# Third norm taken on token rows, router logits from the raw residual, and the first expert's rows gathered by 0/1 matmuls in a two-layer hybrid decoder step

## What is computed

```python
def layer_norm(x, g, b):
    mu = jnp.mean(xf, axis=-1, keepdims=True)
    var = jnp.mean(jnp.square(xf - mu), axis=-1, keepdims=True)
    y = (xf - mu) * lax.rsqrt(var + LN_EPS) * g + b

def moe_swiglu(x, w_router, w_gu, w_down):
    logits = (x @ w_router).astype(jnp.float32)
    top_v, top_i = lax.top_k(logits, TOP_K)
    gates = jax.nn.softmax(top_v, axis=-1)
    ...
    for e in range(N_EXPERTS):
        y = y + swiglu(x, w_gu[e], w_down[e]) * combine[..., e:e + 1]
```

## Time and profile before

| | |
|---|---|
| median of 3 runs | 1705.26 us (1704.07 to 1706.66) |
| the profiled execution's own time | 1708.3 us |
| its span | 1706.4 us |
| PE busy, matmuls / weight loads | 1584.2 us / 1377.1 us |
| DVE / ACT / POOL busy | 1245.2 / 1058.4 / 92.0 us |
| output projection's last matmul ends | at 639.86 us |
| first expert matmul starts | at 688.17 us |

### The profile page before, as it was taken

The page is one execution under the profiler, slowest core; times in us unless marked ns, Lnnn a source line. Parts: engine busy times, 40 slices in busy tenths (PEclk is TensorE's granted clock), DMA queues, the critical chain, the costliest instruction groups (busy, mean ns, idle before and its releaser), DMA issues.

```text
span 1706.4 us, 23448 instructions
## 1 busy us (share of the span) xinstructions
PE 1584.2 (93%) x8917; PEld 1377.1 (81%) x8917; DVE 1245.2 (73%) x1155; ACT 1058.4 (62%) x976; POOL 92.0 (5%) x142
## 2 busy tenths in 40 slices
PE   7999998799996994999999999999999999999992
PEld 6889997699996994787887887887887887887881
DVE  5685444467544653688888888888888888888887
ACT  3981414566434334677877777777777777777772
POOL 3104100011000002000000000000000000002001
PEclk9997998899998997899999999999999999999996
DMA  9646702489552552799999999999999999999991
GB/s 254 212 137 200 279 2 87 131 270 298 203 187 75 173 174 103 280 376 364 360 380 343 382 376 338 391 367 346 390 365 351 385 367 351 384 366 352 396 376 71
DMA packets 228128, 479.65 MB, mean 281 GB/s; under 512 B 9644, under 2 KB 69052, under 8 KB 227769
## 3 DMA queue, kind: packets, MB, share of 16 engines
q1 hardware_dynamic: 215904, 438.92, 72.0%
q0 software_dynamic: 10640, 37.96, 6.4%
q10 hardware_dynamic: 1528, 1.98, 0.4%
...
...
## 4 chain that ended last, share of the span: by engine, by line
PE 87%; ACT 6%; DVE 4%; DMA 1%; issue 1%; POOL 0%; DVEq 0%; SPq 0%; ACTq 0%; POOLq 0%
PE bank L1741 12%; PE bank L1742 12%; PE bank L1745 12%; PE bank L1770 11%; PE bank L342 6%; PE bank L343 6%; PE bank L347 6%; PE bank L1776 6%; ACT high L323 2%; PE bank L1656 1%; PE bank L1657 1%; PE bank L1525 1%; PE bank L1662 1%; PE bank L1546 1%; DVE low L328 1%; PE bank L1753 1%
## 5 line engine op out<-in xcount | busy, mean ns | idle before, releaser
L328 DVE TENSOR_TENSOR low<-raw,high 128x2048 fp32r<-128x2048 f32 x408 | 932.7, 2291 | 279.3 <-ACT high L323 279.3
L323 ACT ACTIVATE high<-raw 128x2048 fp32r<-128x2048 f32 x408 | 781.9, 1918 | 297.2 <-PE bank L1745 108.0
L1741 PE MATMUL bank<-high,xgh 128*128 128x512 f32 x896 | 360.4, 402 | 1.6 <-DVE xgl L1328 1.6
L1742 PE MATMUL bank<-high,xgl 128*128 128x512 f32 x896 | 356.4, 398 | 0.0
L1745 PE MATMUL bank<-low,xgh 128*128 128x512 f32 x896 | 246.7, 397 | 0.0
L342 PE MATMUL bank<-xh,high 128*128 128x264 f32 x864 | 231.0, 300 | 16.8 <-ACT xh L774 9.3
L343 PE MATMUL bank<-xl,high 128*128 128x264 f32 x864 | 227.6, 296 | 0.0
L1745 PEld LDWEIGHTS bank<-low,xgh 128*128 128x128 f32 x896 | 169.8, 190 | 41.2
L1741 PEld LDWEIGHTS bank<-high,xgh 128*128 128x128 f32 x896 | 169.9, 190 | 40.5 <-issue 2.0
L1742 PEld LDWEIGHTS bank<-high,xgl 128*128 128x128 f32 x896 | 169.5, 189 | 38.6
L342 PEld LDWEIGHTS bank<-xh,high 128*128 128x128 f32 x864 | 173.2, 200 | 19.3 <-ACT xh L774 9.7
(11 more groups left out here) (347 smaller groups left out, 1424.6 us busy)
## 6 DMA issues: line engine op xcount, KB each, us to landing
...
```

Of the source, the lines that this page charges most:

```text
L323: eng.activation(high[:, n % SPLIT, :], raw[:, n % RAW, :], ACT.Copy).then_inc(high_ready, 1)
L328: eng.tensor_tensor(low[:, n % RAW, :], raw[:, n % RAW, :], high[:, n % SPLIT, :].bitcast(F32), ALU.subtract).then_inc(low_ready, 1)
L1741: pe.matmul(out, xgh[:, 4 * kh + k, :], wh[:, k, :], start=kh + k == 0, stop=False)
L1742: pe.matmul(out, xgl[:, 4 * kh + k, :], wh[:, k, :], start=False, stop=False)
```

## The change

It does the following.

- **Norm on rows.** PE transposes the un-normed residual into token rows (`row_tiles`, 24 transposes): the first 12 ahead of the last output slot, 6 after it, 6 after the last residual add. DVE takes mean and variance of each row with `bn_stats` (`row_stats`), ACT computes the inverse root, DVE the product `nmr`, and ACT writes `xn` = row * rstd + nmr, without gain and bias. `layer_norm(2)` goes.
- **Logits from the raw residual.** POOL multiplies the router's weights by the norm's gain and bias once, early (`gbw`); PE sums them over the channels with 8 matmuls against ones (`sgb`), ahead of the output slots; the logits are (raw residual x `gbw`) * rstd + nmr * `sgb` part + bias part.
- **First expert by matmul.** DVE compares seat numbers with each token's seat of expert 0 (`onehot`, 0/1), and 24 fp32 matmuls `xn` x `onehot` put the rows into the banks where the transposes of `xrow` used to. The scatter stays, and SP waits for it only at unit 3 of the first job.
- **Gain and bias later.** `tok` now holds rows without gain and bias, so `gathered` first multiplies and adds on DVE (`xf`, 8 operations for each of the jobs), then ACT copies and DVE subtracts. DVE also makes `acc` (6 operations) just before the loop, where ACT did it in one.
- **Filler.** `keep_running` issues transposes of the identity whose results nobody reads: 24, 12 and 20 of them.
- **Rest.** DVE's `low` for the loop's third slot moves behind the ranking; ACT's program has explicit table loads ahead of its norms, before `deltaT`, and at the end; POOL loads gain and bias rows in the short convolution's stage, where ACT did so after the third norm; the last `flag` operation waits for `y_sb` instead of the stored `ysb`.

```diff
                     last = pe.matmul(out, wl[:, k, f], act_h[:, k, :], start=False, stop=k == KT - 1)
             last.then_inc(slot_used, 1)
 
...
+                            sp_.wait_ge(scattered, 96)
...
+            sp_.dma_start(tok[bass.ds(final + 1, 1), :, :].rearrange("a p d -> p (a d)"), ysb[:, :]).then_inc(y_last, 16)
...
+            for i in range(2):
+                pool.wait_ge(ss_out[i], 64)
+            pool.wait_ge(tail_out, 32)
+            for l, at in ((0, vec2_g), (1, vec_g)):
+                pool.dma_start(at[:, :], ln_g[1, l:l + 1, :].to_broadcast([128, D])).then_inc(vec_in, 16)
+            for l, at in ((0, vec2_b), (1, vec_b)):
+                pool.dma_start(at[:, :], ln_b[1, l:l + 1, :].to_broadcast([128, D])).then_inc(vec_in, 16)
+            for a in range(2):
+                ins = pool.tensor_tensor(gbw[:, :, a, :], wr[:, :, :], vecs[:, :, 4 * a + 2:4 * a + 3].to_broadcast([128, KT, EX]),
+                                         ALU.mult)
+            ins.then_inc(const_ready, 1)
...
-            pool.wait_ge(slot_used, MOE0)
+            pool.wait_ge(yl_ready, 8)
...
+            pool.wait_ge(slot_used, MOE0)
...
+            pool.wait_ge(y_sb, final * 2 + 4)
             step(pool.tensor_tensor(flag[:, 3:4], flag[:, 0:1], flag[:, 1:2], ALU.add))
             step.wait()
+            pool.wait_ge(y_last, 16)
...
             act.activation(zgate[:, :, :], zgate[:, :, :], ACT.Copy, scale=norm_w[:, 0:1]).then_inc(z_ready, 1)
...
@@ -826,28 +860,26 @@
             for n in range(SCO0, MOE0):
                 act.wait_ge(slot_used, n + 1)
                 split_high(act, n + SPLIT)
...
-            layer_norm(2, False)
-
-            act.dma_start(vec_g[:, :], ln_g[1, 1:2, :].to_broadcast([128, D])).then_inc(vec_in, 16)
-            act.dma_start(vec_b[:, :], ln_b[1, 1:2, :].to_broadcast([128, D])).then_inc(vec_in, 16)
-            act.wait_ge(pool_step, 4 + 2 * LEVELS + 5)
-            for i in range(6):
-                act.wait_ge(xn_psum, i + 1)
-                p = 128 if i < 4 else 8
-                act.activation(xn[0:p, i // 2, 512 * (i % 2):512 * (i % 2) + 512], bank[i][0:p, :], ACT.Copy)\
-                    .then_inc(xn_ready, 1)
+            act.preload_act_table_set("natural_log")
+            act.wait_ge(var_ready, 1)
+            act.activation(rstd_n[:, :], moments[:, :, 1], ACT.Ln, bias=eps[:, 1:2]).then_inc(log_ready, 1)
+            act.wait_ge(log_ready, 1)
+            act.activation(rstd_n[:, :], rstd_n[:, :], ACT.Exp, scale=-0.5).then_inc(rstd_ready, 1)
+            act.wait_ge(nmr_ready, 1)
+            act.wait_ge(const_ready, 8)
+            for tt in range(3):
+                for h in range(2):
+                    p = 128 if tt < 2 else NS
+                    act.activation(xn[0:p, tt, 512 * h:512 * h + 512], bank[row_bank(tt, h)][0:p, :], ACT.Identity,
+                                   scale=rstd_n[0:p, tt:tt + 1], bias=nmr[0:p, tt:tt + 1]).then_inc(xn_ready, 1)
             act.wait_ge(top_ready, 1)
             act.activation(gates[:, :, :], gates[:, :, :], ACT.Exp).then_inc(ex_ready, 1)
-            act.wait_ge(xn_ready, 6)
-            act.activation(acc[:, :, :], xn[:, :, :], ACT.Copy, scale=ALPHA).then_inc(acc_ready, 1)
 
             def gathered(jobs):
                 for g in range(2):
-                    act.wait_ge(xg_psum, jobs * 2 + (g + 1))
-                    act.activation(xgh[:, 4 * g:4 * g + 4, :], heads(2 + g), ACT.Copy).then_inc(xgh_ready, 1)
-
-            act.wait_ge(scattered, 96)
-            act.dma_start(xrow[:, :], tok[1]).then_inc(xrow_in, 16)
...
@@ -1239,17 +1272,42 @@
                     dve.tensor_tensor(yl[:, f, :], sy[:, 2 * (i % 2) + t, :], yh[:, f, :].bitcast(F32), ALU.subtract)\
                         .then_inc(yl_ready, 1)
                 split_low(dve, n + SPLIT)
+            def row_stats(h):
+                for tt in range(3):
+                    p = 128 if tt < 2 else NS
+                    dve.wait_ge(xn_psum, 3 * h + tt + 1)
+                    step(dve.bn_stats(stats[0:p, tt, h, :], bank[row_bank(tt, h)][0:p, :]))
+
             for n in range(SCO0, MOE0):
                 dve.wait_ge(slot_used, n + 1)
                 for t in range(2):
                     add_residual(2 * (n - SCO0) + t, 2 * ((n - SCO0) % 2) + t)
-                split_low(dve, n + SPLIT)
-            layer_norm(2, False)
-
+                if n < MOE0 - 1:
+                    split_low(dve, n + SPLIT)
+                if n == SCO0:
+                    dve.wait_ge(sgb_psum, 1)
+                    step(dve.tensor_copy(sgb[:, :, :], bank[7][:, 0:16].rearrange("p (a e) -> p a e", a=2)))
+                if n == SCO0 + 2:
+                    row_stats(0)
+            dve.wait_ge(const_ready, 8)
+            row_stats(1)
+            step.wait()
+            for tt in range(3):
+                p = 128 if tt < 2 else NS
+                ins = dve.bn_aggr(moments[0:p, tt, :], stats[0:p, tt, :, :].rearrange("p g s -> p (g s)"))
+            ins.then_inc(var_ready, 1)
+            dve.wait_ge(var_ready, 1)
+            dve.wait_ge(rstd_ready, 1)
+            dve.scalar_tensor_tensor(nmr[:, :], moments[:, :, 0], -1.0, rstd_n[:, :], ALU.mult, ALU.mult).then_inc(nmr_ready, 1)
+            dve.wait_ge(nmr_ready, 1)
+            for tt in range(3):
+                step(dve.scalar_tensor_tensor(over[:, 0, tt, :], sgb[:, 0, :], nmr[:, tt:tt + 1], sgb[:, 1, :], ALU.mult, ALU.add))
             dve.wait_ge(logit_psum, 1)
-            dve.wait_ge(const_ready, 7)
-            step(dve.tensor_copy(logits[:, 0:2, :], bank[6][:, 0:16].rearrange("p (t e) -> p t e", t=2)))
-            step(dve.tensor_copy(logits[0:8, 2, :], bank[6][0:8, 16:24]))
+            step.wait()
+            for tt in range(3):
+                p = 128 if tt < 2 else NS
+                step(dve.scalar_tensor_tensor(logits[0:p, tt, :], bank[2][0:p, 8 * tt:8 * tt + 8], rstd_n[0:p, tt:tt + 1],
+                                              over[0:p, 0, tt, :], ALU.mult, ALU.add))
             step.wait()
             step(dve.tensor_reduce(top[:, :], logits[:, :, :], X, ALU.max))
...
+            step(dve.tensor_reduce(most[:, 0:1], bank[3][:, 24:32], X, ALU.max))
             step.wait()
             for k in range(1, TILES):
...
             step(dve.tensor_tensor(first_at[:, :, :], first_at[:, :, :], last_at[:, :, :], ALU.add))
             step(dve.tensor_reduce(row_f[:, 1, :], last_at[:, :, :], X, ALU.max))
             step.wait()
...
+                    dve.wait_ge(xg_psum, jobs * 2 + (g + 1))
+                    for d in range(4 * g, 4 * g + 4):
+                        ins = dve.tensor_scalar(xf[:, d, :], heads(2 + g)[:, d % 4, :], vecs[:, d, 2:3], vecs[:, d, 6:7],
+                                                ALU.mult, ALU.add)
+                    ins.then_inc(xf_ready, 1)
+                for g in range(2):
                     dve.wait_ge(xgh_ready, jobs * 2 + (g + 1))
-                    dve.tensor_tensor(xgl[:, 4 * g:4 * g + 4, :], heads(2 + g), xgh[:, 4 * g:4 * g + 4, :].bitcast(F32),
+                    dve.tensor_tensor(xgl[:, 4 * g:4 * g + 4, :], xf[:, 4 * g:4 * g + 4, :], xgh[:, 4 * g:4 * g + 4, :].bitcast(F32),
                                       ALU.subtract).then_inc(xgl_ready, 1)
 
             gathered(0)
+            for tt in range(3):
+                step(dve.scalar_tensor_tensor(acc[:, tt, :], xn[:, tt, :], ALPHA, vec2_g[:, :], ALU.mult, ALU.mult))
+            step.wait()
+            for tt in range(3):
+                step(dve.scalar_tensor_tensor(acc[:, tt, :], vec2_b[:, :], ALPHA, acc[:, tt, :], ALU.mult, ALU.add))
             tiles = dve.value_load(rounds_i[0:1, 0:1], min_val=1, max_val=TILES)
             with dve.Fori(0, tiles) as t:
...
                     pe.wait_ge(res_ready, 16 + 2 * i - 2)
+                if i == 3:
+                    pe.wait_ge(stail_sb, 2)
+                    row_tiles(0)
+                    row_tiles(2)
                 dense_slot(pe, n, 2 * (i % 2), yh, yl)
-            pe.wait_ge(stail_sb, 2)
-            layer_norm(2)
-
-            pe.wait_ge(x_new, 24)
+            pe.wait_ge(res_ready, 22)
+            row_tiles(4)
+            pe.wait_ge(res_ready, 24)
+            row_tiles(6)
             for tt in range(3):
                 n_tok = 128 if tt < 2 else NS
                 for k in range(KT):
-                    last = pe.matmul(bank[6][0:n_tok, 8 * tt:8 * tt + 8], xres[:, k, 128 * tt:128 * tt + n_tok], wr[:, k, :],
+                    last = pe.matmul(bank[2][0:n_tok, 8 * tt:8 * tt + 8], xres[:, k, 128 * tt:128 * tt + n_tok], gbw[:, k, 0, :],
                                      start=k == 0, stop=k == KT - 1)
             last.then_inc(logit_psum, 1)
-            for i in range(6):
-                tt, n_tok = i // 2, (128 if i < 4 else NS)
-                for t in range(4):
-                    last = pe.transpose(bank[i][0:n_tok, 128 * t:128 * t + 128],
```

(19 more changed lines are left out.)

67 lines of the change are left out of this document (54 added, 13 removed).

## The result

The changed kernel takes **1690.86 us** (median of 4 runs, 1687.96 to 1691.15) against 1705.68 (median of 4, 1704.07 to 1706.66): a ratio of **0.9911, 95% interval 0.9897 to 0.9925**, a gain of 14.8 us (12.8 to 17.6). The forecast was 1677, with a range of 1669 to 1688. The sign was right. The size was not, and the result lies 3 us outside the range.

The account below looks back on a forecast made before the run. TensorE, with 87% of the chain, was taken as the bound, losing most in a 48.3 us chain before the expert loop. Savings of 21.9 + 2.3 + 1.3 + 2.7 = 28.2 us from 1705.26 gave 1677, range 1669 to 1688.

Parts of the forecast that it names:

- sign: Whole kernel: faster, chance 0.95; same 0.02, slower 0.03.
- 0/1 matmuls, "5.4, to 20.9": First expert's 48 passes take 5.4 us, ending 20.9 us after the last output slot's end.
- Rival 2: Filler doesn't count: after the logits the clock stays at 0.50 into the 0/1 matmuls; 7 us less, 1684; chance 0.2.
- Chain up to the 0/1 matmuls, 15.5: From the last output slot's end through logits, ranking, filler and counts to the 0/1 matmuls: 15.5 us.
- Rule on the filler: The skill's rule that full clock does not engage for transposes; by it the filler would hold nothing.
- Clock at the loop's start, 2.3 us "taken whole": Expert loop's start: about 12 matmuls no longer at half clock, 12 x 0.2 = 2.3 us saved.
- Ahead of the last slot, -3.0: `sgb` sums (1.7 us) and 12 transposes (1.3 us) make the last output slot end 3.0 us later.
- Loop, zero: Expert loop's job ends: added `xf` operations cost nothing, 3.7 us of slack covering them with 0.6 us left.
- Rivals 3, 4 and 5: Job ends stall a little, 1681 to 1685 (0.13); slower there, 1713 (0.03); no gain in the stage, 1701 (0.02).
- DeltaNet, 1.3: DeltaNet stage: one table load of 1.28 us leaves the way to the copy of `P`, 1.3 us saved.
- Tail, 2.7: Program's end: the flag operation starts with the last store, so the gather starts earlier, 2.7 us saved.

Follow-up runs that it names:

- e5_no_filler: The changed kernel with the 0/1 matmuls over 128 rows (e2_full_rows), without any of the 56 filler transposes; 1690.64 us, ratio 0.9906.
- e2_full_rows: The changed kernel with the third token tile's 0/1 matmuls over all 128 rows instead of 8; 1682.37 us, ratio 0.9863.
- e6_before_tail: The kernel before with the change's last part alone, the flag computed while y is being stored; 1703.1 us, ratio 0.998.
- e12_before_tail_again: e6_before_tail measured again beside new runs of the kernel before; 1706.11 us against 1706.39, ratio 0.9994.

## Why the prediction was off, point by point

- **0/1 matmuls, "5.4, to 20.9": failed.** It took 13.32 us, because the price was taken from products over 128 rows while a third of the passes have 8. Over 128 rows the same term measures 5.60. These 7.9 us, the filler's half-clock passes behind it, which end 1.3 us beyond the last `xgl`, and an `xgl` that is done 2.8 us after the last pass and not 2.5, are the 9.6 us by which the chain is too long. None of the rivals had it. Rival 2 had a similar number (1684) and a low clock in the 0/1 matmuls too, but from filler that doesn't count, which `e5_no_filler` excludes; its counts, 18 passes at 0.156, are 2.8 us and not 3.1.
- **Chain up to the 0/1 matmuls, 15.5: right,** 15.57, and in part by luck. The clock fell in the middle of the logits, at 639.1, as reasoned from the decode stage. But the logits took 5.0 us where 6.0 had been counted, and the filler behind them 5.0 where 4.1 had been, so that it ends at 11.5 (forecast 11.6). `sel` is ready at 644.94, 9.95 us after the slot's end (forecast 10.9), and the counts start at 646.32: the filler holds them back by 1.4 us, twice the 0.7 of the forecast.
- **Rule on the filler: the trace decides against it here.** The clock came back 4.4 us into the first filler, when TensorE had issued nothing but `pe.transpose` of the identity since the logits, and without filler 8.3 us are lost. The Trainium skill, "TensorE: Matmul & The Clock Gate", Part 4, says that full clock doesn't engage for transposes; with these fp32 transposes it did.
- **Clock at the loop's start, 2.3 us "taken whole": off by 0.9.** It rested on 0/1 matmuls at full clock. (12 x 0.2 is 2.4, and by the rows, 0.44 less 0.226, 2.6.) As it was, four matmuls ran at half; in `e2_full_rows` none, and its loop takes 983.7 us in place of 984.5, against 985.9 before: 2.2 us.
- **Ahead of the last slot, -3.0: -4.4.** The passes cost 1.96 and 1.47 us (forecast 1.7 and 1.3), and the thin ones also drew the clock down into the first output slot. The range named this, the sum left it out.
- **Loop, zero: right,** with the slack used up almost entirely: the `xf` take 0.33 each, not 0.20 to 0.27, and of the two `low` that end at 795.44 the first is done by about 793.2, with TensorE wanting it at 793.70. Rivals 3, 4 and 5 are out.
- **DeltaNet, 1.3: 3.06,** since the shorter wait also spared the fall of the clock. The 1.0 us between there and the `su` transposes is no gain of the change: that stretch takes 361.37 to 362.17 us in the traces of the changed kernel and its variants, and 361.74 to 362.35 in those of `before`, `e6_before_tail` and `e12_before_tail_again`.
- **Tail, 2.7: failed.** The step "the gather starts at about 1680.1, so all 2.7 count" took the flag's 3.50 us for its own price. Undisturbed it takes 0.19 (`e6_before_tail`). The gather does start 3.05 us earlier behind the copy of `y`, but it inherits the hold, and 0.4 us are left. On top, the copy of `y` now starts 3.4 us behind TensorE's last matmul in place of 1.4, behind two `low` that were pushed back by the `xf` of a job that doesn't exist. Together the tail is 1.35 us longer.
